# Prompt attention: value products of split operands with channels on partitions, output turns gone, 1/sum applied on POOL

## What is computed

```python
def fox_prompt(q, k, v, logf):
    ft = jnp.swapaxes(jnp.cumsum(logf, axis=1), 1, 2)
    scale = HEAD_DIM ** -0.5
    for blk in range(s_len // Q_BLOCK):           # 8 blocks of 128 queries
        q0, q1 = blk * Q_BLOCK, (blk + 1) * Q_BLOCK
        s = jnp.einsum('bqhd,bkhd->bhqk', q[:, q0:q1], k[:, :q1]) * scale
        s = s + ft[:, :, q0:q1, None] - ft[:, :, None, :q1]
        mask = jnp.arange(q1)[None, :] <= jnp.arange(q0, q1)[:, None]
        p = jax.nn.softmax(jnp.where(mask, s, -jnp.inf), axis=-1)
        outs.append(jnp.einsum('bhqk,bkhd->bqhd', p.astype(v.dtype), v[:, :q1]))
    return jnp.concatenate(outs, axis=1)
```

## Time and profile before

| | us |
|---|---|
| median of 3 runs | 3509.45 (3507.27 to 3514.05) |
| profiled execution, its own time | 3501.92 |
| its span, first to last instruction | 3499.8 |
| PE busy in the span | 3356.5 (96%) |
| POOL busy in the span | 716.0 (20%) |
| prompt attention, PE's first turn to its last | 2066 to 2388 |

### The profile page before, as it was taken

How to read it: one execution, slowest core, us unless ns; L and a number is a source line. 1 busy time by engine, 2 the same in 40 slices (tenths; PEclk the granted TensorE clock), 3 DMA queues, 4 the chain that set the end, 5 groups by cost and what they waited for, 6 DMA issues and landing times.

```text
span 3499.8 us, 54119 instructions
## 1 busy us (share of the span) xinstructions
PE 3356.5 (96%) x21295; PEld 3194.3 (91%) x21295; DVE 1275.1 (36%) x2801; ACT 946.1 (27%) x1390; POOL 716.0 (20%) x334
## 2 busy tenths in 40 slices
PE   5999999999989999999999989999999999999997
PEld 3999999999969999998877988889989999999996
DVE  5322222222376155242222227674334222332225
ACT  3111111111143333244343326562122111111112
POOL 1222222222201121111110222221113222322220
PEclk7999999999999999999999999999999999999998
DMA  6223222221122231247767634334111111111101
GB/s 209 89 94 98 93 87 96 86 94 36 37 80 74 77 100 58 94 138 255 249 232 254 216 116 103 87 84 176 59 37 61 36 36 36 48 36 52 44 12 55
DMA packets 251494, 343.24 MB, mean 98 GB/s; under 512 B 39549, under 2 KB 189493, under 8 KB 251122
## 3 DMA queue, kind: packets, MB, share of 16 engines
q1 hardware_dynamic: 224946, 308.41, 27.5%
q10 hardware_dynamic: 26432, 33.18, 2.6%
HBM read 293.54 MB, written 48.01 MB: 98 GB/s over the span
## 4 chain that ended last, share of the span: by engine, by line
PE 90%; DVE 4%; ACT 3%; issue 2%; DMA 1%; ACTq 0%; SPq 0%; DVEq 0%
PE psum L288 26%; PE psum L292 25%; PE psum L291 25%; PE psum L1934 3%; PE psum L1914 2%; PE psum L1497 1%; PE psum L470 1%; PE psum L1544 1%; DVE h_f L674 1%; PE psum L1511 1%; PE psum L1146 1%; PE psum L1901 1%; PE psum L1902 1%; DVE psum L669 1%; ACT acts_hi L715 1%
## 5 line engine op out<-in xcount | busy, mean ns | idle before, releaser
L288 PE MATMUL psum<-acts_hi,w_hi 128*128 128x384 f32 x4032 | 1390.0, 345 | 35.0 <-DVE past_rows L324 23.5
L292 PE MATMUL psum<-acts_hi,w_lo 128*128 128x384 f32 x4032 | 1356.9, 337 | 0.0
L291 PE MATMUL psum<-acts_lo,w_hi 128*128 128x384 f32 x4032 | 1356.5, 336 | 0.0
L288 PEld LDWEIGHTS psum<-acts_hi,w_hi 128*128 128x128 f32 x4032 | 759.8, 188 | 72.4 <-issue 56.3
L291 PEld LDWEIGHTS psum<-acts_lo,w_hi 128*128 128x128 f32 x4032 | 760.3, 189 | 3.3
L278 POOL TENSOR_TENSOR w_lo<-w_raw,w_hi 128x2048 fp32r<-128x2048 f32 x106 | 490.5, 4634 | 1332.6 <-ACT w_hi L272 1332.6
L292 PEld LDWEIGHTS psum<-acts_hi,w_lo 128*128 128x128 f32 x4032 | 759.3, 188 | 0.0
L952 DVE TENSOR_TENSOR u_f<-psum,gated 128x384 f32<-128x384 f32 x132 | 73.6, 557 | 1043.0 <-ACT gated L898 1043.0
L985 DVE SCALAR_TENSOR_TENSOR x<-psum,mods,x 128x384 f32<-128x384 f32 (+1 forms) x552 | 314.7, 570 | 189.2 <-PE psum L292 189.2
L272 ACT ACTIVATE w_hi<-w_raw 128x2048 fp32r<-128x2048 f32 x106 | 200.5, 1909 | 626.5 <-PE psum L288 592.2
L288 PE MATMUL psum<-u_hi,w_hi 128*128 128x384 f32 x1056 | 355.3, 336 | 0.0
(11 more groups left out here) (236 smaller groups left out, 2812.8 us busy)
## 6 DMA issues: line engine op xcount, KB each, us to landing
w_raw<-in_ffn_w SPq DMA_DIRECT2D x66, 1024.0 KB, 5.3
kc<-in_cache_k SPq DMA_DIRECT2D x32, 1024.0 KB, 6.5
vc<-in_cache_v SPq DMA_DIRECT2D x16, 2048.0 KB, 7.9
w_raw<-in_w_ada SPq DMA_DIRECT2D x28, 1024.0 KB, 5.0
w_raw<-in_w_in SPq DMA_DIRECT2D x28, 1024.0 KB, 5.4
sp<-sample_bias SPq DMA_DIRECT2D x128, 65.0 KB, 2.5
ada_w<-in_w_ada SPq DMA_DIRECT2D x4, 2048.0 KB, 15.6
w_raw<-in_w_ada_f SPq DMA_DIRECT2D x8, 1024.0 KB, 5.4
```

The source lines that it names most:

```text
L288: pass1 = eng.matmul(out, whi, ahi, start=first, stop=False)
L291: eng.matmul(out, whi, alo, start=False, stop=False)
L292: return eng.matmul(out, wlo, ahi, start=False, stop=last)
```

## The change

It rewrites the value side of the prompt attention and what hangs on it.

- The values are split too. POOL writes `vs`, which holds for every key the rounded half and the rest of the 64 channels side by side (`split_values`, two instructions per head). `vs` is now the stationary operand, and the turned probabilities of two query blocks (256 columns) are the moving one, first their rounded half, then the rest (`values`, `low` false and true). The output has channels on partitions: one half of them is the sum for the rounded values, the other half that for the rest.
- Every block of turned probabilities is now read twice: ACT copies it rounded (`pT_hi`), DVE writes the difference (`pT_lo`). `pT_hi` and `pT_lo` take the places of the split weight blocks `w_hi` and `w_lo`, and `vs` that of `w_raw1`. The unit is at most four blocks, one bank; units alternate between two banks.
- DVE copies the products of 256 queries from PSUM into `ou` (`output`). A DMA moves the half that belongs to the rest to the other partitions (`lw`), POOL adds the halves (`add_low`), multiplies with 1/sum (`scale_pair`) and splits the pair into `acts_hi` and `acts_lo` (`pair`). The turns of `att` and their splits on DVE are gone.
- 1/sum is taken once per head (`inverse`), stored to DRAM with queries along a row and loaded back for 64 partitions (`rb`).
- The maximum is taken as a minimum of negated scores: the query is scaled with a negative factor, the bias is summed with the other sign and the exponential has scale -1. The negation on DVE is gone, here and in the sample attention.
- SP's order per head is new: `kbias` of the next head, `vh` of the next head behind the split of this head's values (`v_split`), `kf` and `qf`, and then three transfers of the head before (`moved`). The first head's `kbias` and `vh` are loaded in the branch stage.
- The first block of `w_br_att` is split only behind the last values, its rest on DVE; the second is loaded there, as its place holds `vs`. The merge begins with seven of eight pairs of one weight tile and takes the last pair behind them. `z1` from its fourth tile on and the second gate tile wait for the last pair.

The diff, cut to its core:

```diff
+    QUARTERS = 8
+    UNITS_BEFORE = (0, 1, 2, 3, 4, 6, 8, 10)
+    HEAD_UNITS = 12
+    vs_ = [v[:].rearrange("p (k n) -> p k n", n=128) for v in vs]
+    pT_hi = [w[:].rearrange("p (k n) -> p k n", n=256) for w in w_hi[0:2]]
+    pT_lo = [w[:].rearrange("p (k n) -> p k n", n=256) for w in w_lo[0:2]]
+    def units_of(i, k):
+        first = i * 2 * HEAD_UNITS + (HEAD_UNITS * (k // 8) + UNITS_BEFORE[k % 8])
+        return [(first + n, 4 * n, min(4 * n + 4, k % 8 + 1)) for n in range(k % 8 // 4 + 1)]
+    def bank_of(k, n):
+        return 4 + (UNITS_BEFORE[k % 8] + n) % 2
...
+        def moved(i, hh):
+            hd = i * 2 + hh
+            rows = slice(64 * hh, 64 * hh + 64)
+            other = slice(64 - 64 * hh, 128 - 64 * hh)
+            eng.wait_ge(sem("pa_rec"), hd + 1 + 2)
+            eng.dma_start(rec_dram[ds(hd, 1), :].rearrange("o (q p) -> p (o q)", p=128), srec[:, hh, :], allow_slow_non_contiguous=True).then_inc(sem("rec_stored"), 16)
+            eng.wait_ge(sem("a_lo"), NC + 1)
+            eng.wait_ge(sem("pair_scaled"), i + 1)
+            eng.wait_ge(sem("rec_stored"), hd * 16 + 16 + 32)
+            eng.dma_start(rb[rows, :], rec_dram[ds(hd, 1), :].to_broadcast([64, TP])).then_inc(sem("rb_loaded"), 16)
+            eng.wait_ge(sem("pa_o"), i * 8 + 4 * hh + 4 + 2)
+            eng.wait_ge(sem("pair_split"), i + 1)
+            eng.dma_start(lw[rows, :], ou[hh][other, :]).then_inc(sem(f"lw_loaded{hh}"), 16)
+        def body(i, first=False, last=False):
+            for hh in range(2):
+                hd = i * 2 + hh
+                if not (last and hh == 1):
+                    nh = 1 - hh
+                    eng.wait_ge(sem("pa_max"), i * 16 + 8 * hh + 16)
+                    head_bias(eng, hd + 1, nh)
+                    eng.wait_ge(sem("v_split"), 2 * hd + 2)
+                    head_values(eng, hd + 1, nh)
+                    eng.wait_ge(sem("pa_split"), hd + 2)
+                    head_loads(eng, i, hh + 1)
+                if not (first and hh == 0):
+                    moved(i if hh else i - 1, 1 - hh)
...
+        def values(i, q, low):
+            j, hh = q % 4, q // 4
+            done = i * 2 * HEAD_UNITS + (HEAD_UNITS * hh + (UNITS_BEFORE + (HEAD_UNITS,))[2 * j + 2])
+            if not low:
+                if j == 0:
+                    eng.wait_ge(sem("v_split"), i * 4 + 2 * hh + 2)
+                eng.wait_ge(sem("pa_o"), i * 8 + q - 2 + 1 + 2)
+                eng.wait_ge(sem("pa_h"), done)
+            else:
+                eng.wait_ge(sem("pa_l"), done + 2)
+            probs = (pT_lo if low else pT_hi)[q % 2]
+            n = 2 * j + 2
+            for kb in range(n):
+                q0 = 128 if kb == n - 1 else 0
+                last = eng.matmul(ps[6 + q % 2][:, q0:256], vs_[hh][:, kb, :], probs[:, kb, q0:256],
+                                  start=(not low and kb == 0), stop=(low and kb == n - 1))
+            last.then_inc(sem("pa_vl" if low else "pa_vh"), 1)
...
-                eng.activation(pT[k % 2][:, 0:cols], ps[4][:, 0:cols], ACT.Copy).then_inc(sem("pa_c4"), 1)
+                hh, qi = k // 8, k % 8
+                q = k // 2
+                for n, (e, k0, k1) in enumerate(units_of(i, k)):
+                    eng.wait_ge(sem("pa_t"), e + 1)
+                    if not (first and q < 2):
+                        eng.wait_ge(sem("pa_vh"), i * 8 + q - 1)
+                    eng.activation(pT_hi[q % 2][:, k0:k1, 128 * (qi % 2):128 * (qi % 2) + 128],
+                                   ps[bank_of(k, n)][:, 0:128 * (k1 - k0)].rearrange("p (k n) -> p k n", n=128),
+                                   ACT.Copy).then_inc(sem("pa_h"), 1)
                 if k == 1:
...
+        pair_split(eng, B_BRA, 0)
+        last = PAIRS - 1
+        eng.wait_ge(sem("pair_scaled"), PAIRS + 1)
+        eng.activation(acts_hi[:, last, 0:TP], lw[:], ACT.Copy).then_inc(sem("pair_hi"), 1)
...
+    def split_values(eng, i, hd, hh, first=False):
+        main, rest = slice(64 * hh, 64 * hh + 64), slice(64 - 64 * hh, 128 - 64 * hh)
+        eng.wait_ge(sem(f"vh_loaded{hh}"), i * 16 + 16)
+        if not first:
+            eng.wait_ge(sem("pa_vl"), hd * 4 - 4)
+        eng.tensor_tensor(vs_[hh][:, :, main], vh[hh][:], ones[:, 0:HD].unsqueeze(1).to_broadcast([128, TP // 128, HD]), ALU.mult).then_inc(sem("v_split"), 1)
+        eng.wait_ge(sem("v_split"), 2 * hd + 1)
+        eng.tensor_tensor(vs_[hh][:, :, rest], vh[hh][:], vs_[hh][:, :, main].bitcast(F32), ALU.subtract).then_inc(sem("v_split"), 1)
+    def add_low(eng, i, hh):
+        hd = i * 2 + hh
+        rows = slice(64 * hh, 64 * hh + 64)
+        eng.wait_ge(sem(f"lw_loaded{hh}"), i * 16 + 16)
+        return eng.tensor_tensor(lw[rows, :], ou[hh][rows, :], lw[rows, :], ALU.add).then_inc(sem("pair_added"), 1)
+    def scale_pair(eng, i):
+        eng.wait_ge(sem("pair_added"), i * 2 + 2)
+        eng.wait_ge(sem("rb_loaded"), i * 32 + 32)
+        eng.tensor_tensor(lw[:], lw[:], rb[:], ALU.mult).then_inc(sem("pair_scaled"), 1)
+        eng.wait_ge(sem("pair_scaled"), i + 2)
...
+        def pair(i):
+            scale_pair(eng, i)
+            hi = acts_hi[:, ds(i, 1), 0:TP].rearrange("p o t -> p (o t)")
+            lo = acts_lo[:, ds(i, 1), 0:TP].rearrange("p o t -> p (o t)")
+            eng.tensor_copy(hi, lw[:]).then_inc(sem("pair_hi"), 1)
+            eng.wait_ge(sem("pair_hi"), i + 1)
+            eng.tensor_tensor(lo, lw[:], hi.bitcast(F32), ALU.subtract).then_inc(sem("pair_split"), 1)
+        def body(i, first=False, last=False):
+            split_head_lo(eng, i * 2 + 1, 1)
+            split_values(eng, i, i * 2 + 1, 1, first=first)
+            if not first:
+                eng.wait_ge(sem("v_split"), i * 4 + 4)
+                add_low(eng, i - 1, 1)
+                pair(i - 1)
+                eng.wait_ge(sem("pair_split"), i + 1)
+            if not last:
+                split_head_lo(eng, i * 2 + 2, 0)
+                split_values(eng, i + 1, i * 2 + 2, 0)
+            if not last:
+                eng.wait_ge(sem("v_split"), i * 4 + 6)
+            add_low(eng, i, 0)
+            if not last:
+                eng.wait_ge(sem("pair_added"), i * 2 + 1)
+        body(0, first=True)
+        with eng.Fori(1, PAIRS - 1) as i:
+            body(i)
+        body(PAIRS - 1, last=True)
...
+        def lows(i, k, first):
+            qi, q = k % 8, k // 2
+            for n, (e, k0, k1) in enumerate(units_of(i, k)):
+                eng.wait_ge(sem("pa_h"), e + 1)
+                if not (first and q < 2):
+                    eng.wait_ge(sem("pa_vl"), i * 8 + q - 1)
+                cols_ = slice(128 * (qi % 2), 128 * (qi % 2) + 128)
+                eng.tensor_tensor(pT_lo[q % 2][:, k0:k1, cols_],
+                                  ps[bank_of(k, n)][:, 0:128 * (k1 - k0)].rearrange("p (k n) -> p k n", n=128),
+                                  pT_hi[q % 2][:, k0:k1, cols_].bitcast(F32), ALU.subtract).then_inc(sem("pa_l"), 1)
+        def output(i, q, first=False):
+            hh, j = q // 4, q % 4
+            eng.wait_ge(sem("pa_vl"), i * 8 + q + 1)
+            if j == 0 and not first:
+                eng.wait_ge(sem("pair_added"), i * 2 + hh - 1)
+            eng.tensor_copy(ou[hh][:, 256 * j:256 * j + 256], ps[6 + q % 2][:, 0:256]).then_inc(sem("pa_o"), 1)
+        def inverse(i, hh):
+            hd = i * 2 + hh
+            eng.wait_ge(sem("pa_exp"), i * 16 + 8 * hh + 8)
+            eng.wait_ge(sem("rec_stored"), hd * 16 - 16 + 32)
+            eng.reciprocal(srec[:, hh, :], ssum[:, hh, :]).then_inc(sem("pa_rec"), 1)
...
-        split_att(PAIRS - 1, 7)
+        last = PAIRS - 1
+        inverse(last, 1)
+        eng.wait_ge(sem("w_hi_done"), B_BRA + 1)
+        eng.tensor_tensor(w_lo[PAIR_SLOTS[0][2]][:], w_raw[PAIR_SLOTS[0][0]][:], w_hi[PAIR_SLOTS[0][2]][:].bitcast(F32),
+                          ALU.subtract).then_inc(sem("w_lo_done"), 1)
+        output(last, 6)
+        output(last, 7)
+        add_low(eng, last, 1)
+        scale_pair(eng, last)
+        eng.wait_ge(sem("pair_hi"), PAIRS)
+        eng.tensor_tensor(acts_lo[:, last, 0:TP], lw[:], acts_hi[:, last, 0:TP].bitcast(F32), ALU.subtract).then_inc(sem("pair_split"), 1)
...
-            load_block(eng, B_BRA + j, PAIR_SLOTS[j], pair_block("w_br_att")(j))
+        load_block(eng, B_BRA, PAIR_SLOTS[0], pair_block("w_br_att")(0))
...
+        eng.wait_ge(sem("pa_vl"), 8 * PAIRS)
+        load_block(eng, B_BRA + 1, PAIR_SLOTS[1], pair_block("w_br_att")(1))
...
+                            eng.wait_ge(sem("a_lo"), NC + 1)
                     else:
...
                         wait_block(eng, block0 + j)
                     whi, wlo = wcols(PAIR_SLOTS[j % 2][2], t)
-                    for k in range(KT):
+                    late = (block0, j, t) == (B_BRA, 0, 0)
+                    for k in range(KT - late):
                         last = mm3(eng, ps[n][:, 0:CH], whi[k], wlo[k], acts_hi[:, k, tokens_of(c)],
```

(38 more changed lines are left out.)

235 lines of the change are left out of this document (88 added, 147 removed).

## The result

The changed kernel took 3572.6 us (median; 3570.2 to 3579.6), beside 3510.0 for the kernel before on the same chip: a ratio of 1.0181, 95% interval 1.0162 to 1.0199. It is slower by 1.8%, where 0.4% less had been forecast, and outside the range given. The profiled execution has a span of 3568.4 us, 68.6 more than before.

What follows compares the result with a forecast made beforehand. PE set the pace before; afterwards the loop of loading the next head would, at 19.4 us against 20.04. Savings of 1.8 us at the start, 9.0 in the loop and 3.0 at the end: 13.8 off 3509.45, 3495.7 us; range 3462 to 3520.

Steps and rivals of the forecast that it cites:

- the loop of loading the next head: Attention, once per head through ACT, POOL, SP and DMA: from 14.3 us to 19.4, longer than the engines' 16.6.
- break-even: Attention: loop time per head from which the change would lose, 20.4 us, given 4.8 us gained at start and end.
- the slower rival: Attention: next head's loads land as at the first head, loop 21.2 us, 3521 us in all; chance 0.20.
- for 1.75 MB between them that is 9.7 us: Next head's loads: time until the last of six transfers lands, taken between 8.44 us for 1.5 MB and 13.62 for 2.5.
- the upper bound: Next head's loads: 11.5 us to landing if the six transfers go as at the first head; loop 21.2 us.
- I count nothing, 1 us per head at worst: Store of 1/sum on SP, 1024 pieces of 4 bytes: SP past its waits before the next kbias is due, no cost.
- the handshakes that were allowed for: Loop per head: 0.2 us added for handshakes (0.1 us) and some loss to dips of the clock.
- a forecast 33.9: End of the attention, last split to merge: 33.9 us against 36.97 before, a gain of 3.0 us.
- The last pair's sum, scaling and split lie beside 63 matmuls: Merge: last pair's work covered by seven other pairs' matmuls, some 10 us; without cover some 3 us added.
- The start: Second head's split: to begin at 2070.3 instead of 2072.07, 1.8 us sooner; bound for this, nothing.
- the first rival: Attention: loads don't bind, the engines' 16.6 us per head holds, 52 us gained, 3457 us; chance 0.20.
- the sums of 14.4 and 15.5: Attention: work per head in us after the change, DVE 14.4 and ACT 15.5, both under PE's 16.6.

Runs made afterwards that it cites:

- second experiment: Changed kernel with the store of 1/sum laid out as 128 runs of 32 bytes instead of 1024 pieces of 4 bytes: 3518.4 us, 1.0030 of the kernel before.
- third experiment: Changed kernel with keys and queries issued first on SP and 1/sum stored as 128 runs of 32 bytes: 3449.0 us, 0.9830 of the kernel before.

## Why the prediction was wrong

**The mechanism was right.** The step named as deciding, the loop of loading the next head, decides, and ACT's split shows it as forecast, with idle time that a DMA of `qf` ends. The sign hung on the loop's size: break-even was put at 20.4 us, the forecast at 19.4, the slower rival at 21.2; it is 24.2. The slower rival was the right case, and it was still 3 us per head too short.

**First failed step: "for 1.75 MB between them that is 9.7 us".** From `kbias` to the split it takes 11.2 us in the mean even when the store is out of the way (the second experiment). That is close to the upper bound, the first head's 11.5. I took the lower value because two more transfers stood right behind the first head's, and that was no reason: in the changed kernel's own first head `kbias` goes out at 2062.60 and the split begins at 2074.44, 11.8 us, with nothing issued behind these loads in that time. The interpolation went by bytes and left out their order. With keys and queries first and the store out of the way, the same six transfers land within 9.6 us of the first issue (third experiment, mean of 14 heads), which is what I had forecast; with `kbias` and `vh` first it takes 11.1 (second experiment). The miss is 1.5 us per head, 21 us. The Trainium skill (DMA: Bandwidth & Descriptors, Queues, rings and completion order) has descriptors taken in ring order; the 11.2 us agree with what I had drawn from it. By the same reading of mine the loads should also have been safe from a store issued behind them, and there the 7.1 us for a last `qf` that takes 5.4 without the store speak against it. The measurement decides.

**Second failed step: "I count nothing, 1 us per head at worst".** The store of 1/sum cost 2.9 us per head in the landing of the loads (14.1 against 11.2), 41 us in all. I had the nearest row, `vh` with as many pieces, and read from it only how late the store itself would be, and whether SP would be free again; that SP would be was right in the changed order. I did not ask what 1024 pieces do to the loads in flight beside them. With the store issued 3.4 us behind the last `qf`, it falls in the middle of their landing in every head. What it delays is not the bytes. By the trace's records of DMA packets, the last packet of the loads ends 7.3 us behind the issue of the last `qf` in the changed kernel and 7.2 in the second experiment; but the semaphore that tells of the landing comes 3.6 us behind that packet, against 0.8 (means of 14 heads). In the head shown above, and in the second experiment's, nothing moves any more in these stretches (DMA share 0.00, 0 GB/s), and the last `qf` lands at 2126.57 and 2202.95, just behind them:

```profile
2121.10:2126.50 5.40, 0.00 (x0) 0.00 (x0) 0.00 (x0) 0.00 (x0) 0.00 (x0) 0.71 0.00 0
...
2202.30:2202.90 0.60, 0.00 (x0) 0.00 (x0) 0.00 (x0) 0.00 (x0) 0.00 (x0) 1.00 0.00 0
```

In nine of the 14 heads the loads' landing is told less than 0.9 us ahead of the store's own. The Trainium skill (DMA: Bandwidth & Descriptors, Rules for kernel authors) says that a strided last dimension becomes one descriptor per element and is better rearranged; the traces agree: in the same place, 9.1 us in the median for this store against 4.6 in runs of 32 bytes (second experiment).

**Smaller terms.** `kbias` goes out 10.15 us behind the split, not 9.5, 0.45 us past the handshakes that were allowed for. With the two above this is 4.8 us per head, the whole difference of 24.23 and 19.4. From the last split to the merge 34.2 us came of a forecast 33.9. "The last pair's sum, scaling and split lie beside 63 matmuls" failed: store and `lw` took 9.28 and 4.65 us in a row, and the 3 us named as the price without that cover came out as 3.5; the merge's gates, queued on SP behind them, added 4.1 that I had not listed. The start lost 2.4 us instead of gaining 1.8: the loads were issued 2.0 us later than before (2062.60 against 2060.56), as the stage ahead ended later, and landed no sooner.

**What held.** With the loop freed the first rival's price is there: 16.41 us per head, 16.6 forecast, and 3449 us, 3457 forecast. In the middle 200 us of that run DVE and ACT are busy for 13.1 and 13.4 us per head (159.69 and 163.64 times 16.41 over 200); the sums of 14.4 and 15.5 were somewhat high, as they added pipelined instructions end to end. That 16.41 and 16.6 lie so close is partly luck: the granted clock there is 1.00, where it was 0.97 in the same 200 us of the kernel before, and the forecast did not count on that. The saved matmuls are real; the change lost them again in the loop through SP's queue.

Shown by the runs: that each of order and store costs what is said here, that the loop is free only with both mended (the order, and the store's pieces or SP's wait for it), and that in the changed kernel the store delays the telling of the loads' landing and not their packets. Why pieces of 4 bytes hold it back, and why the order of the six transfers matters, no run here shows; that stays open.

## What to carry to other kernels

When a change puts transfers or waits in front of others on a queue, follow the loop that goes around through that queue once per iteration and price it at the slowest comparable landing in the trace, above all if the sign turns within the bounds. A store of a few kilobytes is priced by its pieces, not its bytes, and three times over: its own landing, the loads in flight beside it, and everything queued behind whoever waits for it. Issue first what the next iteration's first step reads, and lay small results out so that one partition's values lie side by side; the reader can turn the order around for less than a microsecond.

## What the runs showed of the hardware

A store of 1024 pieces of 4 bytes lands 9.1 us after its issue in the changed kernel's median; the same 4 KB as 128 pieces of 32 bytes lands in 4.6 in the same place, and in 1.5 where keys and queries go out first and the loads have landed by then. Issued 0.64 us behind a load of 256 KB, the first kind stretches the landing of that load from 5.4 us to 7.1 in the median, though it was issued later. In the changed kernel the packets of the loads end as early with either store (7.3 and 7.2 us behind the last issue), and the landing follows after 3.6 us with the first kind and after 0.8 with the second. Among the versions of the changed kernel, which do the same work per head, the granted clock is the higher the less PE waits: 0.84 with 131 us of PE in 200, 0.93 with 158, 1.00 with 181. Busy time alone does not set it: the kernel before has 0.97 with 184.
